# Hybrid decoder layer (HGRN2 and gated delta rule): one VectorE product moved two steps ahead in the delta loop, and one state load moved ahead in GpSimd's queue

## The chip, the cores and the metric

The kernel runs on one core of a Trainium2 chip. The metric is the device time in microseconds (us), the median of several runs; lower is better. Engines are named as in the profile: PE is TensorE (matmul) and PEld its weight load, DVE is VectorE, ACT is ScalarE, POOL is GpSimd, SP is the queue that issues the weight loads.

## The reference, cut to what matters

One inference step of one decoder layer, for a prompt of 256 tokens and for 8 samples of 4 tokens (288 token columns together), model width 2048, float32. An input projection feeds an HGRN2 branch (16 heads) and a gated-delta branch (16 query/key heads, 32 value heads of 128x128 state); the branches are merged, projected, and followed by a feed-forward block. Around the change stands the gated delta branch:

```python
conv = jax.nn.silu(conv)                         # causal width-4 convolution on q, k, v
beta = jax.nn.sigmoid(gb)
o_gdn, s_gdn_new = gdn_scan(q_g, k_g, v_g, log_a, beta, s_gdn.astype(f32))
o_gdn = rmsnorm(o_gdn, gdn_norm_g) * jax.nn.silu(gz.reshape(B, T, GDN_V_HEADS, GDN_DV))
...
X = lax.linalg.triangular_solve(A + eye, rhs, left_side=True, lower=True, unit_diagonal=True)
u, w = X[..., :GDN_DV], X[..., GDN_DV:]
v_new = u - jnp.einsum('bhtd,bhdv->bhtv', w, S)
```

`silu(gz)` is the output gate of the delta branch; `s_gdn` is the recurrent state that the samples bring along.

## The kernel before

Everything is transposed: 128 channels on the partitions, the 288 tokens as columns. A *slab* is one output block of 128 channels: 16 contraction tiles, each with three matmuls (`products`, L609 to L611), since float32 is split into a high and a low part (`hi*hi + lo*hi + hi*lo`). Weights come in *pieces* of 128x512: SP loads them in pairs into `raw` (8 pieces), ScalarE rounds them to `whi` (`split_hi`, L1036), VectorE subtracts to get `wlo` (`split_lo`, L1530); `whi` and `wlo` hold 4 pieces, and the splits run 3 pieces ahead of TensorE.

The heads' own work is woven by hand between the matmuls. Each slab has 8 *steps* `s`; the six slabs of one delta iteration have steps 0 to 47. For every step each engine's program says what it does there: `delta_first` and `delta_second` on TensorE, `delta_own` (the head pair `n+1` that is being projected) and `delta_prev` (the pair `n` whose scan runs) on ScalarE and VectorE; on both of these a step is `delta_prev`, then `delta_own`, then, at even steps, one weight split. Every engine works off its own program in order, and semaphores tie them together. There are 16 head pairs: an iteration without a scan (`S_G0`), eight iterations (`S_G1`), a stage of other slabs (`S_WB1`), seven iterations (`S_G2`), and the last pair's scan in the stage of the gates (`S_GB0`), where the split comes ahead of `delta_prev`.

The triangular solve is a chain of five levels. At level `l` TensorE makes `g_PU` (L799, at steps 4, 8, 11, 14, 17) from `glev` and `g_Ui`, ScalarE copies it, TensorE makes the correction (L812, and L815 for the samples), VectorE subtracts it from `g_Ui` (L1890, with L1889 for the samples, at steps 6, 10, 12, 16, 19) and transposes (L1893). GpSimd makes `glev` (L2338), the level's part of `g_A`.

The gate `silu(gz)` has two parts for each head pair. For the second, ScalarE computes the sigmoid at step 4 (`sigmoid_z(2 * n + 2)`), and VectorE multiplies at step 7 (`silu_z`, L1872, 128x288, both inputs in SBUF). Its result is read at step 42; it frees `g_ca` and `g_ce` for the convolution that starts at step 10. In between, at step 5, VectorE copies the halo of the convolution into `g_U` (L1774).

GpSimd runs its own program and issues DMAs in the same queue. In the stage `S_WA`, in which the HGRN2 output is projected, it stores finished blocks (`save`, L2239) and loads gates (`load_gate`, L2251); this stage also carries a share of the adaLN products, with weights of its own (`in_w_ada`). At its end GpSimd issues what the delta stage needs: `load_cache` (three small DMAs, L2277), `load_delta` (two DMAs of 512 KB, L2294, the samples' states `g_S0` of a head pair), `decay_rows` and `own` (which has the products L2317 and L2329). TensorE reads `g_S0` from step 9 of an iteration on.

Of the kernel before, what the change touches and what calls it, by code (L numbers as in the profile page):

```python
# [118 lines left out]
def hybrid_layer(nc, x_prompt, x_sample, state_hgrn, state_gdn, cache_conv, c_prompt, c_sample, lb_logits,  # L119
# [70 lines left out]
    with ExitStack() as ctx:  # L190
# [1251 lines left out]
        def _(dve):  # L1442
# [325 lines left out]
            def head(t, i, size=1):  # L1768
                return t[:, i:i + size] if isinstance(i, int) else t[:, bass.ds(i, size)]
# [99 lines left out]
            def silu_z(m, k):  # L1869

                dve.wait_ge(sg["g_zrec"], EARLIER + m)
                tt_(gz[:, k, :], gca[:, 0:T], gce[:, 0:T], MUL).then_inc(sg["g_z"], 1)  # L1872
# [1 line left out]
            UNEW = (6, 10, 12, 16, 19)  # L1874

            def delta_prev(s, n, slot):
                if s == 7:
                    silu_z(2 * n + 2, 1)
                if s == 12:
                    dve.wait_ge(sg["g_qws"], n + 1)  # L1880
                    tt_(guTs[:, :, :].rearrange("p e (b t) -> p e b t", t=TS), R[7][:, 64:128].rearrange("p (e b t) -> p e b t", e=2, t=TS),
                        gqws[:, :, :, 1, :], ADD).then_inc(sg["g_vt"], 1)
                if s in UNEW:
                    l = UNEW.index(s) + 1
                    dve.wait_ge(sg["g_ut"], 5 * n + l)
                    dve.wait_ge(sg["g_u1"], EARLIER + n + 1)
                    dve.wait_ge(sg["g_unew"], 5 * n + l - 1)
                    if l == 1:
                        tt_(gUs[0:NS, :, :], gUs[0:NS, :, :], R[4][0:NS, 0:2 * NS].rearrange("p (e s) -> p e s", s=NS), SUB)  # L1889
                    tt_(gUi[:, :, :], gUi[:, :, :], R[2][:, :].rearrange("p (q s) -> p q s", s=P), SUB).then_inc(sg["g_unew"], 1)  # L1890
                    if l < 5:
                        dve.wait_ge(sg["g_unew"], 5 * n + l)
                        flip(gT[:, :, :].rearrange("p q s -> p (q s)"), gUi[:, :, :].rearrange("p q s -> p (q s)")).then_inc(sg["g_tnew"], 1)  # L1893
                if s in (19, 23):
                    e = (s - 19) // 4
                    dve.wait_ge(sg["g_dss"], 2 * n + e + 1)
                    dve.wait_ge(sg["g_sdec"], 2 * n + e + 1)
                    for a in range(2):
                        h_ = gS0[:, e, 4 * a:4 * a + 4, :]
                        last = tt_(h_, h_, R[4 + a][:, :].rearrange("p (b v) -> p b v", v=P), ADD)  # L1900
                    last.then_inc(sg["g_snew"], 1)
                if s in DS:
                    c = DS.index(s)
                    dve.wait_ge(sg["g_ds"], 4 * n + c + 1)
                    dve.wait_ge(sg["g_o"], n)
                    dve.wait_ge(sg["g_stored"], 16 * n)
                    dve.wait_ge(sg["g_st"], 4 * n + c)
                    for e in range(2):
                        add = R[5][:, 2 * P * (c % 2) + e * P:2 * P * (c % 2) + (e + 1) * P]
                        if c == 0:  # L1910
                            last = copy(gS[:, 0, e, :], add)
                        else:
                            last = stt(gS[:, c, e, :], gS[:, c - 1, e, :], gsc[:, e, 9 + c:10 + c], add, MUL, ADD)
                    last.then_inc(sg["g_st"], 1)
                if s == 36:
                    dve.wait_ge(sg["g_ocp"], EARLIER + n + 1)
                    for e in range(2):
                        last = tt_(go[:, e, TP:T].rearrange("p (b t) -> p b t", t=TS),
                                   (R[7], R[4])[e][:, TP:T].rearrange("p (b t) -> p b t", t=TS), gqws[:, e, :, 0, :], ADD)
                    last.then_inc(sg["g_oadd"], 1)  # L1920
                if s == 42:
                    dve.wait_ge(sg["g_ors"], n + 1)
                    dve.wait_ge(sg["g_ohi"], n)
                    dve.wait_ge(sg["g_oadd"], EARLIER + n + 1)
                    dve.wait_ge(sg["g_z"], 2 * (n + 1))
                    stt(go[:, :, :], go[:, :, :], vec[:, 0, 6 * KT + 1:6 * KT + 2], gn1[:, :, :], MUL, MUL).then_inc(sg["g_ot1"], 1)
                    dve.wait_ge(sg["g_ot1"], EARLIER + n + 1)
                    tt_(gn2[:, :, :], go[:, :, :], gz[:, :, :], MUL).then_inc(sg["g_out"], 1)
                if s == 43:
                    dve.wait_ge(sg["g_ohi"], n + 1)  # L1930
                    tt_(head(olo, 2 * slot, 2), gn2[:, :, :], head(ohi, 2 * slot, 2).bitcast(F32), SUB).then_inc(sg["g_olo"], 1)

            def delta(at, j, n, slot):
                for s in range(49):
                    if n is not None:
                        delta_prev(s, n, slot)
                    delta_own(at, s, j)
                    if s % 2 == 0 and s < 48:
                        split_lo(at, s // 2)
# [12 lines left out]
            for s in range(49):  # L1952
                if s % 2 == 0 and s < 48:
                    split_lo(pos(S_GB0), s // 2)
                delta_prev(s, GJ - 1, HALF - 1)
# [176 lines left out]
        def _(pool):  # L2132
# [104 lines left out]
            def save(t, j, k):  # L2237

                pool.dma_start(scratch(t, j), pb[:, k, :]).then_inc(sg[f"t_stored{k}"], 16)  # L2239
# [16 lines left out]
            def merged_out(n):  # L2256
                at = pos(S_WA, n, 2)
                for k in range(2):
                    pool.wait_ge(sg[f"acc_free{at.bank(k)}"], at.drained(k))
                    save(merged_d, 2 * n - 2 + k, k)  # L2260
                    load_gate(2 * n + k, k)
# [5 lines left out]
            def conv_cols(t, j, c):  # L2267
                first, mul, size = cols[c]
                v = t.rearrange("r (c p) -> r c p", p=P)
                return v[:, first + mul * j:first + mul * j + size, :] if isinstance(j, int) else \  # L2270
                    v[:, bass.ds(first + mul * j, size), :]
# [3 lines left out]
            def load_cache(j):  # L2275
                for c in range(3):
                    pool.dma_start(gcc[0:24, places[c], :], conv_cols(cache_conv[0].rearrange("b s c -> (b s) c"), j, c)  # L2277
                                   ).then_inc(sg["g_cc"], 16)
# [8 lines left out]
            def pair_of(t, j):  # L2287

                v = t[0].rearrange("b (j e) d v -> j e d b v", e=2)
                return v[j] if isinstance(j, int) else v[bass.ds(j, 1)].squeeze(0)  # L2290

            def load_delta(j):
                for e in range(2):
                    pool.dma_start(gS0[:, e], pair_of(state_gdn, j)[e]).then_inc(sg["g_s0"], 16)  # L2294
# [77 lines left out]

            pool.wait_ge(sg["g_zero"], 1)
            load_cache(0)
            with pool.Fori(KT // 2 - 2, KT // 2) as n:
                merged_out(n)
            for k in range(2):
                at = pos(S_WA + KT - 2)
                pool.wait_ge(sg[f"acc_free{at.bank(k)}"], at.drained(k) + 1)
                save(merged_d, KT - 2 + k, k)  # L2380
            load_delta(0)
            pool.wait_ge(sg["g_halo_turned"], 1)
            load_cache(1)
            decay_rows(0)
# [89 lines left out]
```

## Time and profile before

| | |
|---|---|
| median of 3 runs | 3541.8 us (3540.53 to 3541.84) |
| the profiled execution: its own time | 3541.8 us |
| its span | 3540.3 us |
| TensorE, matmul | 98% busy |
| VectorE | 63% busy |
| ScalarE | 51% busy |
| GpSimd | 24% busy |
| delta iterations | 1012 to 1604 us and 1740 to 2255 us, the last scan to 2325 us |

The span is the profiled stretch from the first to the last instruction; 1.5 us lie around it. In a timeline row stand the start, the duration, the engine and line, the operation with what it writes and reads, and in brackets how long the engine had been idle before it and what ended that. A row with "x3" is three instructions in a row. Matmuls overlap, so a matmul of 0.29 us is followed by the next after 0.13 us.

### The profile page before, as it was taken

How to read it: one execution, taken by the hardware profiler on the slowest of the kernel's cores; microseconds unless marked ns; L12 is line 12 of the kernel's file. 1: busy time of each engine (PE TensorE's matmuls, PEld its weight loads, DVE VectorE, ACT ScalarE, POOL GpSimd, SP SyncE). 2: the span in 40 equal slices, each digit the busy share in tenths (PEclk: the TensorE clock that was granted, in tenths of full speed). 3: DMA queues.
4: the chain of work that ended last, by engine and by line, in shares of the span. 5: the costliest groups of instructions: out<-in, count | busy, mean ns of one | idle time of the engine just before them, and what ended most of it. 6: DMA issues, size and time to landing. Idle time of an engine off the chain costs nothing.

```text
span 3540.3 us, 76760 instructions
## 1 busy us (share of the span) xinstructions
PE 3475.6 (98%) x24605; PEld 3173.3 (90%) x24605; DVE 2236.2 (63%) x4307; ACT 1796.9 (51%) x3735; POOL 846.5 (24%) x995
## 2 busy tenths in 40 slices
PE   9999999999999999999999999999989999999998
PEld 2599999998889999998899999999879889999998
DVE  2476666746677777776677777646666665555555
ACT  1245454555545555556555555454665555344454
POOL 2122222211144554541254554412000000000000
PEclk9999999999999999999999999999999999999999
DMA  8755555567834443448744343468764775555554
GB/s 279 214 151 156 145 160 144 161 175 240 271 110 118 120 112 109 124 123 239 210 119 128 111 122 108 122 185 249 232 188 138 223 232 166 166 161 165 161 165 139
DMA packets 884547, 588.09 MB, mean 166 GB/s; under 512 B 23427, under 2 KB 816037, under 8 KB 884165
## 3 DMA queue, kind: packets, MB, share of 16 engines
q1 hardware_dynamic: 857828, 510.50, 50.5%
q0 software_dynamic: 26624, 76.41, 7.6%
q8 instruction: 50, 0.82, 0.1%
q14 instruction: 45, 0.36, 0.0%
HBM read 545.83 MB, written 40.99 MB: 166 GB/s over the span
## 4 chain that ended last, share of the span: by engine, by line
PE 69%; DVE 1%; issue 1%; ACT 1%; DVEq 0%; ACTq 0%
PE acc L609 18%; PE acc L611 17%; PE acc L610 17%; PE bank L799 2%; PE bank L812 2%; PE bank L849 2%; PE bank L833 1%; PE bank L621 1%; PE bank L622 1%; PE bank L870 1%; PE bank L881 1%; PE bank L895 1%; PE bank L771 1%; PE bank L742 1%; PE bank L747 0%
## 5 line engine op out<-in xcount | busy, mean ns | idle before, releaser
L1530 DVE TENSOR_TENSOR wlo<-raw,whi 128x512 fp32r<-128x512 f32 x1799 | 1304.7, 743 | 824.0 <-ACT whi L1036 809.8
L1036 ACT ACTIVATE whi<-raw 128x512 fp32r<-128x512 f32 x1799 | 1093.9, 627 | 838.6 <-PE acc L611 796.3
L609 PE MATMUL acc<-ahi,whi 128*128 128x288 f32 x4112 | 1288.3, 313 | 14.7 <-DVE alo L2041 9.1
L610 PE MATMUL acc<-alo,whi 128*128 128x288 f32 x4112 | 1214.7, 295 | 0.0
L611 PE MATMUL acc<-ahi,wlo 128*128 128x288 f32 x4112 | 1210.9, 294 | 0.0
L609 PEld LDWEIGHTS acc<-ahi,whi 128*128 128x128 f32 x4112 | 775.1, 188 | 37.4 <-issue 26.5
L610 PEld LDWEIGHTS acc<-alo,whi 128*128 128x128 f32 x4112 | 776.1, 189 | 13.3 <-issue 11.5
L611 PEld LDWEIGHTS acc<-ahi,wlo 128*128 128x128 f32 x4112 | 775.4, 189 | 0.0
L609 PE MATMUL acc<-ohi,whi 128*128 128x288 f32 x1792 | 532.7, 297 | 2.1 <-DVE wlo L1530 1.8
L610 PE MATMUL acc<-olo,whi 128*128 128x288 f32 x1792 | 529.3, 295 | 0.0
L611 PE MATMUL acc<-ohi,wlo 128*128 128x288 f32 x1792 | 527.9, 295 | 0.0
L609 PEld LDWEIGHTS acc<-ohi,whi 128*128 128x128 f32 x1792 | 336.6, 188 | 20.0 <-DVE wlo L1530 10.7
L610 PEld LDWEIGHTS acc<-olo,whi 128*128 128x128 f32 x1792 | 337.0, 188 | 2.9
L611 PEld LDWEIGHTS acc<-ohi,wlo 128*128 128x128 f32 x1792 | 337.8, 189 | 0.0
L2338 POOL TENSOR_TENSOR g_lev<-g_A,levm 128x512 f32<-128x512 f32 x80 | 114.8, 1435 | 264.3 <-DVE g_C L1795 220.1
L1787 DVE SCALAR_TENSOR_TENSOR g_ca<-g_U,g_cw,g_ca 128x312 f32<-128x312 f32 x192 | 130.3, 678 | 6.8
L1276 ACT ACTIVATE g_PU<-bank 128x512 f32<-128x512 f32 x80 | 47.9, 599 | 158.4 <-PE bank L799 147.7
L581 PE MATMUL acc<-raw,cst 128*9 128x512 f32 x256 | 116.7, 612 | 4.9 <-DVE cst L1461 2.5
L621 PE MATMUL bank<-whi,cs 128*18 128x512 f32 x256 | 101.4, 396 | 5.1 <-DVE wlo L1530 4.0
L1890 DVE TENSOR_TENSOR g_Ui<-g_Ui,bank 128x512 f32<-128x512 f32 x80 | 54.6, 683 | 80.1 <-PE bank L812 80.1
L581 PEld LDWEIGHTS acc<-raw,cst 128*9 128x9 f32 x256 | 22.4, 92 | 89.2 <-issue 72.0
L622 PE MATMUL bank<-wlo,cs 128*18 128x512 f32 x256 | 101.6, 397 | 0.0
(431 smaller groups left out, 4377.8 us busy)
## 6 DMA issues: line engine op xcount, KB each, us to landing
raw<-in_w_in SPq DMA_DIRECT2D x386, 512.0 KB, 4.1
raw<-in_w_ada SPq DMA_DIRECT2D x192, 512.0 KB, 4.6
raw<-in_w_up SPq DMA_DIRECT2D x128, 512.0 KB, 4.2
raw<-in_w_down SPq DMA_DIRECT2D x128, 512.0 KB, 4.0
raw<-in_w_out_gdn SPq DMA_DIRECT2D x64, 512.0 KB, 5.0
raw<-in_w_o SPq DMA_DIRECT2D x34, 512.0 KB, 4.7
raw<-in_w_out_hg SPq DMA_DIRECT2D x32, 512.0 KB, 5.5
g_S<-in_state_gdn POOLq DMA_DIRECT2D x32, 512.0 KB, 6.5
```

What stands on the lines that cost most here:

```text
L581: last = mm(acc[c % 2][0:NC, :], cst[:, 2 * l + a, :], raw[:, 2 * (l % 4) + a].rearrange("p k c -> p (k c)"), start=(l + a == 0), stop=(l ...
L609: mm(bank[:, 0:T], whi[:, s, r, :], hi[:, kt, :], start=(kt == 0), stop=False, skip_group_check=True)
L610: mm(bank[:, 0:T], whi[:, s, r, :], lo[:, kt, :], start=False, stop=False, skip_group_check=True)
L611: last = mm(bank[:, 0:T], wlo[:, s, r, :], hi[:, kt, :], start=False, stop=(kt == KT - 1), skip_group_check=True)
L621: mm(R[4][0:2 * NC, :], cs2[:, kt, :], whi[:, s].rearrange("p k c -> p (k c)"), start=(kt == 0), stop=False)
L622: mm(R[4][0:2 * NC, :], cs2[:, kt, :], wlo[:, s].rearrange("p k c -> p (k c)"), start=False, stop=(kt == KT - 1)).then_inc(sg["piece_used" ...
L799: last = mm(R[3][:, p * P:(p + 1) * P], glev[:, l % 2, p, :], gUi[:, p, :], start=True, stop=True)
L812: last = mm(R[2][:, p * P:(p + 1) * P], gT[:, p, :], gPU[:, p, :], start=True, stop=True)
L1036: f(whi[:, s], raw[:, r], ACT.Copy).then_inc(sg["hi_made"], 1)
L1530: tt_(wlo[:, s], raw[:, r], whi[:, s].bitcast(F32), SUB).then_inc(sg["lo_made"], 1)
L1787: stt(gca[:, 0:CW], gU[:, k, a:a + CW], gcw[:, k, a:a + 1], gca[:, 0:CW], MUL, ADD).then_inc(sg["g_part" if a < 3 else "g_tap"], 1)
L2338: last = pt(glev[:, l % 2], gA[:, :, :], levm[:, l, :].unsqueeze(1).to_broadcast([P, 4, P]), MUL)
```

## The change

Two edits. VectorE's `silu_z` of the second gate part stands at step 5 of `delta_prev` instead of step 7, so ahead of the halo copy of step 5 and of the update of `g_Us` and `g_Ui` at step 6. GpSimd's `load_delta(0)` stands right behind `load_cache(0)`, ahead of the last two passes of `merged_out` and of the last two saves, instead of behind them.

```diff
             def delta_prev(s, n, slot):
-                if s == 7:
+                if s == 5:
                     silu_z(2 * n + 2, 1)
                 if s == 12:
                     dve.wait_ge(sg["g_qws"], n + 1)
...
             pool.wait_ge(sg["g_zero"], 1)
             load_cache(0)
+            load_delta(0)
             with pool.Fori(KT // 2 - 2, KT // 2) as n:
                 merged_out(n)
             for k in range(2):
                 at = pos(S_WA + KT - 2)
                 pool.wait_ge(sg[f"acc_free{at.bank(k)}"], at.drained(k) + 1)
                 save(merged_d, KT - 2 + k, k)
-            load_delta(0)
             pool.wait_ge(sg["g_halo_turned"], 1)
             load_cache(1)
```

## Rows read from the trace of the kernel before

**Rows 1.** The page, part 1: busy time of each engine.
```profile
PE 3475.6 (98%) x24605; PEld 3173.3 (90%) x24605; DVE 2236.2 (63%) x4307; ACT 1796.9 (51%) x3735; POOL 846.5 (24%) x995
```

**Rows 2.** Waits of TensorE, 905 to 2330 us: total, times, longest.
```profile
PE acc L609 <- DVE wlo L1530: 3.7, 5, 1.4
PE bank L742 <- issue: 2.2, 2, 1.3
...
PE bank L799 <- DVE g_Ui L1890: 0.7, 1, 0.7
```

**Rows 3.** Timeline of VectorE, steps 4 to 7 of one delta iteration.
```profile
1238.59 1.76 DVE L1530 TENSOR_TENSOR wlo<-raw,whi 128x512 fp32r<-128x512 f32 x1 [2.07 <-ACT whi L1036]
1240.28 0.24 DVE L1774 COPY g_U<-bank 128x96 f32<-128x96 f32 x1
...
1240.57 0.67 DVE L1890 TENSOR_TENSOR g_Ui<-g_Ui,bank 128x512 f32<-128x512 f32 x1
...
1242.48 0.45 DVE L1872 TENSOR_TENSOR g_z<-g_ca,g_ce 128x288 f32<-128x288 f32 x1
1244.84 0.69 DVE L1530 TENSOR_TENSOR wlo<-raw,whi 128x512 fp32r<-128x512 f32 x1 [1.91 <-ACT whi L1036]
```

**Rows 4.** Timeline of TensorE, same iteration: step 8.
```profile
1241.77 1.05 PE L799 MATMUL bank<-g_Ui,g_lev 128*128 128x128 f32 x8
```

**Rows 5.** Timeline of GpSimd, same iteration.
```profile
1238.11 1.41 POOL L2329 TENSOR_TENSOR g_at<-g_GR,g_QKm 128x256 f32<-128x256 f32 x2
1239.49 0.31 POOL L2330 TENSOR_TENSOR g_ats<-g_GRs,g_QKms 32x64 f32<-32x64 f32 x1
1239.77 1.72 POOL L2338 TENSOR_TENSOR g_lev<-g_A,levm 128x512 f32<-128x512 f32 x1
```

**Rows 6.** Timeline of VectorE, step 16 of the last scan.
```profile
2280.91 0.67 DVE L1890 TENSOR_TENSOR g_Ui<-g_Ui,bank 128x512 f32<-128x512 f32 x1
```

**Rows 7.** Timeline of TensorE, same place.
```profile
2281.74 1.02 PE L799 MATMUL bank<-g_Ui,g_lev 128*128 128x128 f32 x7 [0.66 <-DVE g_Ui L1890]
```

**Rows 8.** Timeline of VectorE, one head of the HGRN2 stage.
```profile
312.12 0.68 DVE L1530 TENSOR_TENSOR wlo<-raw,whi 128x512 fp32r<-128x512 f32 x1
312.86 0.46 DVE L1665 TENSOR_TENSOR h_X<-h_q,h_E 128x288 f32<-128x288 f32 x1
313.24 1.07 DVE L1666 TENSOR_TENSOR h_X<-h_k,h_E 128x288 f32<-128x288 f32 x1
```

**Rows 9.** Timeline of GpSimd, same place.
```profile
312.91 1.08 POOL L2208 TENSOR_TENSOR h_X<-h_q,h_E 128x288 f32<-128x288 f32 x1 [6.56 <-ACT h_E L1119]
```

**Rows 10.** Timeline of VectorE, end of the first delta iteration.
```profile
1006.00 5.25 DVE L1530 TENSOR_TENSOR wlo<-raw,whi 128x512 fp32r<-128x512 f32 x1
1011.18 0.98 DVE L1872 TENSOR_TENSOR g_z<-g_ca,g_ce 128x288 f32<-128x288 f32 x1
```

**Rows 11.** Timeline of GpSimd, same place.
```profile
1010.67 1.17 POOL L2329 TENSOR_TENSOR g_at<-g_GR,g_QKm 128x256 f32<-128x256 f32 x1
```

**Rows 12.** Timeline of VectorE, end of the second delta iteration.
```profile
1084.21 0.44 DVE L1872 TENSOR_TENSOR g_z<-g_ca,g_ce 128x288 f32<-128x288 f32 x1
1084.58 0.67 DVE L1530 TENSOR_TENSOR wlo<-raw,whi 128x512 fp32r<-128x512 f32 x1
```

**Rows 13.** Timeline of GpSimd, same place.
```profile
1083.42 2.31 POOL L2317 TENSOR_TENSOR g_bek<-g_tk,g_sc 32x256 f32<-32x256 f32 x1
```

**Rows 14.** Timeline of VectorE, step 6 of the first iteration with a scan.
```profile
1018.39 0.21 DVE L1889 TENSOR_TENSOR g_Us<-g_Us,bank 32x64 f32<-32x64 f32 x1 [0.80 <-PE bank L815]
```

**Rows 15.** Timeline of VectorE, step 6 of an iteration in the second half.
```profile
1894.09 0.67 DVE L1890 TENSOR_TENSOR g_Ui<-g_Ui,bank 128x512 f32<-128x512 f32 x1
```

**Rows 16.** Timeline of TensorE, step 8 of the same iteration.
```profile
1895.39 0.83 PE L799 MATMUL bank<-g_Ui,g_lev 128*128 128x128 f32 x6
```

**Rows 17.** Timeline of VectorE, step 6 of the last scan.
```profile
2261.09 1.31 DVE L1530 TENSOR_TENSOR wlo<-raw,whi 128x512 fp32r<-128x512 f32 x1 [1.94 <-ACT whi L1036]
```

**Rows 18.** Timeline of GpSimd, same place.
```profile
2261.81 1.73 POOL L2338 TENSOR_TENSOR g_lev<-g_A,levm 128x512 f32<-128x512 f32 x1
```

**Rows 19.** Timeline of GpSimd, end of the stage S_WA.
```profile
909.85 1.54 POOL L2277 DMA_DIRECT2D g_cc<-in_cache_conv  x3
...
958.73 1.79 POOL L2294 DMA_DIRECT2D g_S<-in_state_gdn  x2
```

**Rows 20.** Busy times by stretch, then granted clock, DMA share, GB/s.
```profile
900.00:935.00 35.00, 34.30 (x231) 29.50 (x231) 23.23 (x39) 19.60 (x34) 5.89 (x11) 1.00 0.90 276
```

## The prediction

> **What bounds the kernel now.** I read the page first: TensorE is busy for 98% of the span [rows 1], so a gain or a loss counts only where it changes one of TensorE's rare gaps. Next came the waits of TensorE from 905 to 2330 us, the stretch that both edits touch. Its gaps there add up to 12.2 us in ten groups, 3.7 us of it for `wlo`, and one wait of 0.7 us, in the whole stretch, for VectorE's update of `g_Ui`, the tile beside which the first edit acts [rows 2]. So neither edit has much to win: even if all 12.2 us went, that would be 0.34% of 3541.8 us. The question is what either can lose. For that I read the timelines of VectorE, TensorE and GpSimd through one iteration of the delta loop (near 1240 us), compared the same place in all 16 iterations, and then looked for other places where VectorE and GpSimd overlap.
>
> **Edit 1: `silu_z(2n+2, 1)` from step 7 to step 5.** It is one `tensor_tensor` of 128x288 with both inputs in SBUF, 0.45 us, 16 times. At step 7 it stands behind the first update of `g_Ui`, at 1242.48 us, and VectorE is then free for 1.9 us until it waits for ACT [rows 3]. At step 5 it stands right behind the `wlo` split of step 4 (1238.59 to 1240.35 us) and ahead of the halo copy (`g_U`) and of the update of `g_Us` and `g_Ui` at step 6. ScalarE's `sigmoid_z` stands ahead of the `whi` piece that this split itself waits for, so no semaphore holds it up. Behind it in VectorE's queue is the `g_Ui` update, and for that TensorE waits: its second group of L799 (step 8) reads the new `g_Ui`.
>
> The slack of that update: it ends at 1240.57 + 0.67 = 1241.24 us and TensorE starts L799 at 1241.77, so 0.53 us [rows 3, 4]. From VectorE's end to TensorE's start when TensorE really waits takes 2281.74 - (2280.91 + 0.67) = 0.16 us [rows 6, 7]. So 0.37 us can be lost for nothing. An undisturbed silu_z takes this much and no more: the next instruction starts 0.37 us after it (1084.21 to 1084.58) [rows 12]. With nothing else in play, edit 1 costs about zero, by a hair.
>
> But GpSimd is in play. Its `g_lev` product (L2338, 128x512) is issued at 1239.77 us, while the split runs, and ends at 1241.49 [rows 5]. The split shows what overlap means: 1.76 us at 1238.59 against 0.68 where GpSimd is quiet [rows 3, 8], since it sat behind the two `g_at` products; it ran from about 1240.35 - 0.68 = 1239.67, and `g_lev`, issued 0.10 us later, waited in turn. Today the next VectorE operations (halo copy, `g_Us`, `g_Ui`) read PSUM and do not mind GpSimd: their 0.24 and 0.67 us are the same with and without it. silu_z has both inputs in SBUF. Who goes first, silu_z or the waiting `g_lev`? The trace of before has both answers.
>
> - GpSimd gets in between. In the HGRN stage L1665 runs from 312.86, GpSimd's L2208 is issued at 312.91, and the next VectorE product (L1666, the same shape as silu_z) takes 1.07 us instead of 0.46: it ends at 314.31, 0.32 us behind GpSimd's 313.99 [rows 8, 9]. This repeats in all 16 heads. And at 1011 us there is the very pair of the new order: a split that had been held up (5.25 us) ends at 1011.25, GpSimd's L2329 had been issued at 1010.67, 0.10 us after the split could start, and silu_z right behind took 0.98 us and ended at 1012.16, again 0.32 us behind GpSimd's 1011.84 [rows 10, 11].
> - VectorE keeps its turn. At 1083.42 GpSimd's L2317 is issued and takes 2.31 us, as a split, silu_z and a split run undisturbed in a row [rows 12, 13]; so in 15 iterations. There GpSimd's product was issued ahead of the first of the three.
>
> In the new place `g_lev` comes 0.10 us after the split could start: as at 1011 us, not as at 1083. I take the first answer. The chip has a rule for this too: the Trainium skill, SBUF — State Buffer, section "Who interferes with whom", says that a VectorE instruction with two SBUF inputs contends with a GpSimd instruction that reads SBUF, and that the second to issue blocks until the first is through. By that rule silu_z, issued at about 1240.28, stands behind `g_lev`, issued at 1239.77; the rows at 312 and 1011 us agree with it, the row at 1083.42 does not. With the rule the sum below comes out at 3557, without it at 3543.
>
> The price then: `g_lev` ends at 1241.49, as now; silu_z at 1241.49 + 0.32 = 1241.81; the halo copy starts 0.07 us before that, at 1241.74, where it starts at 1240.28 today. The shift is 1.46 us. TensorE waits 1.46 + 0.16 - 0.53 = 1.09 us. I find a slack of 0.53 us in five iterations and of 0.60 to 0.63 in seven (1895.39 - 1894.76 = 0.63 in one of them [rows 15, 16]), which makes 1.0 us in these; in one more VectorE has 0.2 us to spare and the wait is 0.8. Sum: 5 x 1.09 + 7 x 1.0 + 0.8 = 13.3 us. The first iteration of each half loop costs nothing: VectorE idles there for 0.80 us before `g_Us` [rows 14], and `g_lev` has already run. The last iteration (in the stage of the gates) has no slack (0.14 us) and another order: silu_z comes ahead of the `wlo` split that today starts at 2261.09 and takes 1.31 us under GpSimd's products [rows 17]. If silu_z runs into those products, the split comes later and can then fall behind `g_lev` of 2261.81 (1.73 us) [rows 18]; I bound it by 0.4 us (silu_z alone) and 1.7 us (behind `g_lev`), and take 1.3. Edit 1: 14.6 us. GpSimd itself is late for nobody: the product it makes at that point is needed some steps later.
>
> Nothing of this is won back at step 7: there VectorE only becomes idle sooner.
>
> **Edit 2: `load_delta(0)` earlier.** Two transfers of 0.52 MB, issued at 958.73 us today, go to about 911.4, right behind the `g_cc` loads of 909.85 [rows 19]. Nobody waits for them: the first reader is step 9 of the second delta iteration, the better part of 60 us behind today's issue. GpSimd pays 1.79 us of issuing, in a time when it waits for the next `pb`; the saves and gate loads behind it are two slabs ahead of their use. What it can cost is bandwidth: the stretch already moves 276 GB/s with the DMA engines 90% busy [rows 20]. Bounds: nothing, if the weights' lead (eight pieces of `raw`, up to four of `whi`/`wlo`) covers it; 1.05 MB / 276 GB/s = 3.8 us, if all of it goes ahead of weights and no lead covers any. I take 1 us, since ScalarE does wait for DMA there but TensorE mostly does not. A gain from a freer DMA after 958 us is bounded by the two waits for L742 that follow (2.2 us [rows 2]); they stand behind ScalarE's and VectorE's convolution work, not behind a transfer, so I take nothing.
>
> **Sum.** The profiled execution took 3541.8 us itself (span 3540.3), the same as the median. 3541.8 + 14.6 + 1.0 = 3557.4, rounded to 3557.
>
> **Rivals.**
> - *VectorE keeps its turn* (as at 1083 us): silu_z costs 0.37 us of shift, all of it slack; at most 0.08 us in each of five iterations and 0.4 us in the last. With edit 2 at 1 us: 3543, no change. The point that decides is whether silu_z in its new place takes 0.45 us or about 1.5. Chance 0.30.
> - *The early load starves the weights* and silu_z is harmless: up to 3.8 us of stalls near 911 to 925 us: 3546, no change within 0.2%. Chance 0.05.
> - *Faster*: what was late is relieved (the L742 gaps of 2.2 us, the 0.7 us wait for `g_Ui`): 3539, which is still no change; all 12.2 us would have to go for 3530. Chance 0.03 for a true gain, by something the trace does not show.
> - *The change does nothing*: if silu_z waited for its sigmoid and the order of VectorE's work stayed as it is; but ScalarE runs that sigmoid ahead of the `whi` piece for which the split of step 4 waits, so this can only be in the last iteration, where the order is another. Contained in the first rival.
>
> **How the numbers follow.** The likeliest case (0.62) gives 3557, with its own range 3551 to 3561: the last iteration and edit 2 at either bound, and 0.1 us on each of 13 waits. The range must take in the no-change case as well: 3541 to 3561. 0.2% (7 us) is what a measurement can tell here. Slower 0.63, same 0.34, faster 0.03.
>
> **What would show it.** Right: L1872 has 13 or so instances of about 1.5 us; TensorE's waits list L799 behind `g_Ui` 13 or 14 times with 1.0 to 1.1 us each; GpSimd's `g_lev` there still takes 1.72 us. Wrong: L1872 stays at 0.45 us and `g_lev` grows to about 2.1 us. Edit 2 is right if the load lands near 920 us and TensorE's gaps from 905 to 960 us grow by no more than 2 us. The prediction fails if the arbitration between the two engines goes by something else than the order of issue, or if the split of step 4 no longer overlaps `g_lev`.

## The result, and the profile after

The changed kernel took 3562.58 us (median of 4 runs, 3558.65 to 3563.32), the kernel before 3541.16 us beside it (4 runs, 3535.44 to 3541.84): a ratio of 1.0064, 95% interval [1.005, 1.0079], 21.4 us slower. The forecast was 3557 us with 3561 at the top of the range: the direction and the mechanism of edit 1 came out as forecast, and the time lies 1.6 us above the range. The forecast was 15.6 us over the 3541.8 us of the time before. The profiled execution took 3563.5 us, with a span of 3562.0 us against 3540.3, 21.7 us more.

The page, part 1, answers to [rows 1]: TensorE is still busy for 98% of a longer span. VectorE's busy time grew by 16.5 us, the first sign of instructions that are held up while they count as running.

```profile
PE 3481.4 (98%) x24605; PEld 3176.9 (89%) x24605; DVE 2252.7 (63%) x4307; ACT 1796.9 (50%) x3735; POOL 845.4 (24%) x995
```

The waits of TensorE from 905 to 2360 us (total, times, longest), which answer to [rows 2]:

```profile
PE bank L799 <- DVE g_Ui L1890: 13.6, 15, 1.5
PE acc L609 <- ACT g_C L1045: 3.3, 1, 3.3
PE acc L609 <- DVE wlo L1530: 2.4, 4, 1.4
PE bank L747 <- DVE wlo L1530: 2.3, 2, 1.1
PE bank L742 <- issue: 2.2, 2, 1.3
```

The wait for `g_Ui` went from 0.7 us once to 13.6 us in 15 waits, the forecast's main sign (one of the 15 is the old one, 0.65 us at 2303.5 us); the wait for L742 is what it was. The 3.3 us behind `g_C` is new, and 1.1 of the 2.3 us at L747 too. VectorE in the iteration of [rows 3], now 3.8 us later:

```profile
1242.41 1.77 DVE L1530 TENSOR_TENSOR wlo<-raw,whi 128x512 fp32r<-128x512 f32 x1 [2.06 <-ACT whi L1036]
1244.10 1.54 DVE L1872 TENSOR_TENSOR g_z<-g_ca,g_ce 128x288 f32<-128x288 f32 x1
1245.56 0.24 DVE L1774 COPY g_U<-bank 128x96 f32<-128x96 f32 x1
...
1245.86 0.67 DVE L1890 TENSOR_TENSOR g_Ui<-g_Ui,bank 128x512 f32<-128x512 f32 x1
```

GpSimd in the same place, answering to [rows 5]:

```profile
1243.32 0.31 POOL L2330 TENSOR_TENSOR g_ats<-g_GRs,g_QKms 32x64 f32<-32x64 f32 x1
1243.60 1.72 POOL L2338 TENSOR_TENSOR g_lev<-g_A,levm 128x512 f32<-128x512 f32 x1
```

`g_lev` still takes 1.72 us and ends at 1245.32; silu_z takes 1.54 us in place of 0.45 and ends at 1245.64, 0.32 us behind it, as the two models at 312 and 1011 us had it [rows 8 to 11]. The halo copy starts 3.15 us behind the split's start, where it was 1.69 us [rows 3]: the shift is the forecast's 1.46 us. Of the 16 silu_z in the new place, 13 take 1.53 to 1.55 us; the first of each half loop takes 0.45 us (1019.30 and 1756.00 us), the one in the last scan 3.09 us.

TensorE's timeline of after, six instructions (the load's stretch, the first L734, the same step 8 as in [rows 4], the last scan):

```profile
921.35 0.40 PE L609 MATMUL acc<-ohi,whi 128*128 128x288 f32 x1 [3.28 <-ACT g_C L1045]
...
962.34 0.60 PE L734 MATMUL bank<-ident,g_cc 128*128 128x128 f32 x4
...
1246.67 1.13 PE L799 MATMUL bank<-g_Ui,g_lev 128*128 128x128 f32 x8 [0.93 <-DVE g_Ui L1890]
...
2274.46 1.05 PE L799 MATMUL bank<-g_Ui,g_lev 128*128 128x128 f32 x8
...
2281.93 1.13 PE L799 MATMUL bank<-g_Ui,g_lev 128*128 128x128 f32 x8 [1.49 <-DVE g_Ui L1890]
...
2292.03 1.05 PE L799 MATMUL bank<-g_Ui,g_lev 128*128 128x128 f32 x8
```

The counterparts of the second, fourth, fifth and sixth of these in the kernel before, the same matmuls:

```profile
960.37 0.60 PE L734 MATMUL bank<-ident,g_cc 128*128 128x128 f32 x4
...
2257.26 1.05 PE L799 MATMUL bank<-g_Ui,g_lev 128*128 128x128 f32 x8
...
2263.26 1.13 PE L799 MATMUL bank<-g_Ui,g_lev 128*128 128x128 f32 x8
...
2270.19 1.13 PE L799 MATMUL bank<-g_Ui,g_lev 128*128 128x128 f32 x8
```

Subtract, and the 21.7 us fall into five pieces. One more pair of the same matmul (an L621 at 883.02 us before, 881.00 after) gives the first:

| stretch (time of before) | shift at its end | share |
|---|---|---|
| up to 883 us | -2.02 | -2.0 |
| 883 to 960: stage with the early load | +1.97 | +4.0 |
| 960 to 2257: the delta iterations | +17.20 | +15.2 |
| 2257 to 2263: the wait in the last scan | +18.67 | +1.5 |
| 2263 to 2270: right behind it | +21.84 | +3.2 |

**The first piece is not the change's.** The profiled execution of before had an interruption of its own: a TensorE wait of 2.30 us at 838.77 us, and a granted clock of 0.88 in the ten microseconds from 840, where after has 1.00. Both kernels run the same code there. In the ten other profiled executions the same matmul too comes 0.7 to 4.5 us earlier than in before. My sum was made against 3541.8 us, which held these 2 us; in the runs beside the experiments below the kernel before takes 3537.7 to 3538.7 us.

**The piece of the early load.** GpSimd issues it at 908.57 us, and ScalarE then gets its next pieces of weights late; timeline of GpSimd, then of ScalarE:

```profile
908.57 1.84 POOL L2294 DMA_DIRECT2D g_S<-in_state_gdn  x2
```

```profile
912.73 1.15 ACT L1036 ACTIVATE whi<-raw 128x512 fp32r<-128x512 f32 x2 [1.04 <-DMA raw<-in_w_ada]
...
919.67 1.15 ACT L1036 ACTIVATE whi<-raw 128x512 fp32r<-128x512 f32 x2 [3.85 <-DMA raw<-in_w_out_hg]
920.73 0.57 ACT L1045 ACTIVATE g_C<-bank 18x512 f32<-18x512 f32 x1
```

TensorE's wait is put down to `g_C`, but the engine that makes `g_C` had itself waited 3.85 us for the DMA of `raw`: that is where the 3.28 us come from. Stretches of after (busy us of PE, PEld, DVE, ACT, POOL, then granted clock, DMA share, GB/s); the first answers to [rows 20]:

```profile
900.00:935.00 35.00, 31.67 (x203) 27.17 (x202) 20.17 (x34) 17.27 (x30) 6.64 (x11) 0.95 0.90 276
910.00:920.00 10.00, 8.07 (x55) 6.84 (x53) 4.37 (x7) 3.47 (x7) 1.53 (x3) 1.00 1.06 311
920.00:930.00 10.00, 8.65 (x51) 7.96 (x52) 5.31 (x10) 4.87 (x9) 1.08 (x2) 0.83 0.76 241
...
2280.00:2290.00 10.00, 8.51 (x49) 8.31 (x48) 3.50 (x6) 3.36 (x7) 5.62 (x9) 0.70 0.29 77
```

In the kernel before, the second of these:

```profile
910.00:920.00 10.00, 10.00 (x70) 8.85 (x69) 7.07 (x12) 6.49 (x12) 2.50 (x5) 1.00 0.96 279
```

Over 35 us the DMA share is 0.90 and the rate 276 GB/s in both kernels. Over the ten microseconds in which the load runs they are 1.06 and 311 GB/s, where before had 0.96 and 279: there was little room left there even without the load. TensorE's clock is granted at 0.83 in the stretch behind the wait, 1.7 of the 4.0 us of this piece, and at 0.70 behind the 1.49 us wait of the last scan (1.00 in before in both). Of its two levels, 2.4 and 1.2 GHz, TensorE had the lower for a part of these stretches, behind a wait in each case.

**The last scan.** VectorE, then GpSimd, answering to [rows 17, 18]:

```profile
2276.28 3.09 DVE L1872 TENSOR_TENSOR g_z<-g_ca,g_ce 128x288 f32<-128x288 f32 x1
2279.30 1.77 DVE L1530 TENSOR_TENSOR wlo<-raw,whi 128x512 fp32r<-128x512 f32 x1
```

```profile
2276.80 0.61 POOL L2317 TENSOR_TENSOR g_kls<-g_tk,g_sc 32x256 f32<-32x256 f32 x1
2277.37 1.40 POOL L2329 TENSOR_TENSOR g_at<-g_GR,g_QKm 128x256 f32<-128x256 f32 x2
2278.74 0.32 POOL L2330 TENSOR_TENSOR g_ats<-g_GRs,g_QKms 32x64 f32<-32x64 f32 x1
```

silu_z does not get in between GpSimd's products at all: it ends at 2279.37, behind the chain up to `g_ats` (2279.06) by 0.31 us.

### The profile page after: what moved, and what is told of

The parts are those of the page before. It is cut to its first block, busy times and chain, and to the rows that moved or that the text cites. A ratio compares the mean times of both kernels' runs of the same rounds, so it can differ in the third digit from the quotient of the medians.

```text
span 3562.0 us, 76760 instructions
## 1 busy us (share of the span) xinstructions
PE 3481.4 (98%) x24605; PEld 3176.9 (89%) x24605; DVE 2252.7 (63%) x4307; ACT 1796.9 (50%) x3735; POOL 845.4 (24%) x995
## 4 chain that ended last, share of the span: by engine, by line
PE 93%; DVE 3%; issue 2%; DMA 1%; ACT 1%; DVEq 0%; POOL 0%; ACTq 0%; SPq 0%; POOLq 0%
PE acc L609 23%; PE acc L611 22%; PE acc L610 22%; PE acc L581 3%; PE bank L799 2%; PE bank L812 2%; PE bank L849 2%; PE bank L833 1%; PE bank L621 1%; PE bank L622 1%; DMA raw<-in_w_ada 1%; PE bank L870 1%; PE bank L674 1%; PE bank L676 1%; DVE wlo L1530 1%
## 5 line engine op out<-in xcount | busy, mean ns | idle before, releaser
L610 PEld LDWEIGHTS acc<-alo,whi 128*128 128x128 f32 x4112 | 776.6, 189 | 13.3 <-issue 11.5
L609 PEld LDWEIGHTS acc<-ohi,whi 128*128 128x128 f32 x1792 | 336.7, 188 | 22.6 <-DVE wlo L1530 10.0
L621 PE MATMUL bank<-whi,cs 128*18 128x512 f32 x256 | 101.3, 396 | 3.4 <-DVE wlo L1530 2.5
L799 PE MATMUL bank<-g_Ui,g_lev 128*128 128x128 f32 x640 | 87.9, 280 | 16.6 <-DVE g_Ui L1890 13.6
```

What stands on the lines that cost most here:

```text
L609: mm(bank[:, 0:T], whi[:, s, r, :], hi[:, kt, :], start=(kt == 0), stop=False, skip_group_check=True)
L610: mm(bank[:, 0:T], whi[:, s, r, :], lo[:, kt, :], start=False, stop=False, skip_group_check=True)
L621: mm(R[4][0:2 * NC, :], cs2[:, kt, :], whi[:, s].rearrange("p k c -> p (k c)"), start=(kt == 0), stop=False)
L799: last = mm(R[3][:, p * P:(p + 1) * P], glev[:, l % 2, p, :], gUi[:, p, :], start=True, stop=True)
```

## Experiments

Each stands beside runs of the kernel before on the same chip, whose medians were 3538.39 us (e1 to e4), 3538.72 (e5 to e8) and 3537.72 (e9, e10).

| run | edit | us (median, runs) | over before | ratio, 95% interval |
|---|---|---|---|---|
| e1 | edit 1 alone | 3555.14 (5) | +16.8 | 1.0049 [1.0035, 1.0062] |
| e2 | edit 2 alone | 3544.89 (11) | +6.5 | 1.002 [1.0011, 1.0029] |
| e3 | PSUM copy of that length instead | 3540.08 (10) | +1.7 | 1.0004 [0.9995, 1.0013] |
| e4 | edit 1, `g_lev` later | 3543.68 (10) | +5.3 | 1.0016 [1.0006, 1.0025] |
| e5 | edit 1 but for the last scan | 3553.8 (5) | +15.1 | 1.004 [1.0026, 1.0054] |
| e6 | half of edit 2 | 3542.67 (11) | +4.0 | 1.0007 [0.9998, 1.0016] |
| e7 | edit 2, 32 us later | 3544.65 (11) | +5.9 | 1.0016 [1.0007, 1.0025] |
| e8 | `g_lev` later alone | 3539.91 (10) | +1.2 | 1.0002 [0.9992, 1.0011] |
| e9 | both edits again | 3560.29 (5) | +22.6 | 1.0066 [1.0052, 1.008] |
| e10 | edit 1, two products | 3563.34 (4) | +25.6 | 1.0069 [1.0053, 1.0084] |

**e1 and e2: each edit alone.**

```diff
e1: -                if s == 7:
    +                if s == 5:
e2: +            load_delta(0)          (behind load_cache(0))
    -            load_delta(0)          (behind the last saves)
```

> Edit 1 alone (silu_z at step 5, the load where it was). Theory (silu_z sits behind GpSimd's g_lev 13 times, each time TensorE waits 0.9 to 1.2 us more, and the last scan loses about 4.6 us with a fall of the clock): 3541.2 + 17 to 18 = 3558 to 3560, L1872 at about 1.5 us in 13 instances. Rival (the early load does most of it, the iterations pay less than the waits say because slack elsewhere gives some back): under 3552.

> Edit 2 alone (load_delta(0) early, silu_z at step 7). Theory (1.05 MB share the DMA engines with the weights where these are 90% busy; TensorE stalls once by about 3.3 us and its clock falls after that): 3541.2 + 4 to 5 = 3545 to 3546, one wait of 3 us or more near 918 us. Rival (the stall at 918 us is an accident of one execution, the load is hidden): 3541 to 3542, no wait above 1 us there.

The two differences of medians, 16.8 and 6.5 us, add to 23.3 where both together cost 21.4 to 22.6: they add up. TensorE's waits, e1 and then e2, and e2's other wait in the same stretch:

```profile
PE bank L799 <- DVE g_Ui L1890: 13.6, 15, 1.5
```

```profile
PE acc L609 <- ACT g_C L1045: 2.8, 1, 2.8
...
915.23 0.40 PE L609 MATMUL acc<-ohi,whi 128*128 128x288 f32 x1 [1.66 <-DVE wlo L1530]
```

e1 has the 13.6 us and no wait for `g_C`, e2 has the wait for `g_C` and still the old 0.7 us for `g_Ui`. e2 refutes my "about 1 us" for the load: its trace loses 5.0 us against before from 883 to 960 us (L621 at 878.51, L734 at 960.88 us), where the profiles without a load there move by -1.1 to +0.6 us, and 1.1 us more at L747, 6.1 us in all, close to the 6.5 us of the medians.

**e3: as long on VectorE, but not on the shared input.** A copy of 128x288 from PSUM into a spare tile at step 5; silu_z stays at step 7.

```diff
+                    copy(spare[:, :], R[7][:, 0:T])
```

> Kernel before, with one more VectorE instruction at step 5, in the place where edit 1 puts silu_z: a copy of 128x288 from PSUM into a spare tile, which takes as long as silu_z (0.45 us) but reads only PSUM. silu_z stays at step 7. Theory (it is the second SBUF input that meets GpSimd): the copy takes 0.45 us, the g_Ui update moves by 0.37 us, inside its slack, TensorE waits for g_Ui no more than 0.1 us an iteration: 3541 to 3543. Rival (any VectorE work of this length ahead of g_Ui costs TensorE about 1 us an iteration): 3553 to 3557.

VectorE of e3, at the place of [rows 3] (its lines stand one or two later):

```profile
1236.78 0.45 DVE L1775 COPY spare<-bank 128x288 f32<-128x288 f32 x1
1237.15 0.24 DVE L1776 COPY g_U<-bank 128x96 f32<-128x96 f32 x1
```

The copy takes 0.45 us while GpSimd's `g_lev` runs from 1236.28 to 1238.01 beside it, and TensorE's wait for `g_Ui` stays at 0.7 us, once. So the slack does cover an undisturbed operation of this length, and silu_z's own 0.37 us is not the cost. What is left is the wait behind `g_lev`.

**e4: edit 1 with `g_lev` moved away,** and **e8: that move alone.** GpSimd issues the three `g_cc` loads first and `g_lev` behind them, 1.6 us later.

```diff
-                level(n, 3)
                 if cache:
                     pool.wait_ge(sg["g_halo_turned"], n + 2)
                     load_cache(n + 2)
+                level(n, 3)
```

> Edit 1 alone, and GpSimd's order changed in prev: load_cache is issued ahead of the product g_lev of level 3 instead of behind it, so that in the 14 iterations with a load_cache no GpSimd product waits beside the split of step 4. Theory: silu_z at step 5 then takes 0.45 us in these iterations and TensorE's waits for g_Ui go from 13 or 14 to 2 (the two iterations without load_cache): 3541 + 5.5 to 6 = 3546 to 3548. Rival (silu_z at step 5 is slow for another reason, its sigmoid for one): no change against edit 1 alone, 3558 to 3560.

> Control: silu_z at step 7 and the load late, as before, but load_cache ahead of g_lev of level 3 in GpSimd's queue. Theory (that order matters only for a VectorE product with two SBUF inputs beside it, and TensorE waits for none of them before): 3537 to 3542, the same as before, so the gain of that order in the run with edit 1 is all from silu_z. Rival (the order is a gain by itself): 3534 or less.

VectorE, then GpSimd, of e4 in the same iteration:

```profile
1236.04 0.81 DVE L1530 TENSOR_TENSOR wlo<-raw,whi 128x512 fp32r<-128x512 f32 x1 [2.06 <-ACT whi L1036]
1236.77 0.97 DVE L1872 TENSOR_TENSOR g_z<-g_ca,g_ce 128x288 f32<-128x288 f32 x1
```

```profile
1235.56 1.86 POOL L2329 TENSOR_TENSOR g_at<-g_GR,g_QKm 128x256 f32<-128x256 f32 x2
1237.39 0.53 POOL L2330 TENSOR_TENSOR g_ats<-g_GRs,g_QKms 32x64 f32<-32x64 f32 x1
```

With `g_lev` gone, silu_z does not get the 0.45 us that I had expected. It falls behind the next product that GpSimd has waiting, here the second of the two `g_at`: that one ends at 1237.42, silu_z at 1237.74, again 0.32 us behind. It takes 0.97 or 0.98 us in 11 of the 16 places, 0.45 in two, 1.53 in two and 3.09 in the last scan. Most of the 0.97 is slack, and TensorE's waits for `g_Ui` are 3.3 us in 4 times. Edit 1's cost falls from 16.8 to 5.3 us, and e8 shows that the move has no gain of its own to lend. In the 11 places the product beside which silu_z lands sets its price. One place does not fit: at 1088.28 us silu_z takes 1.53 us and ends 1.28 us behind the last product of GpSimd, while GpSimd only issues the three `g_cc` loads. The trace does not say what it waited for.

**e5: the last scan at step 7.**

```diff
-                if s == 5:
+                if s == (7 if isinstance(n, int) and n == GJ - 1 else 5):
```

> Edit 1 alone in all iterations, but in the last scan (stage of the gates) silu_z stays at step 7. Theory (the last scan pays its own 1.5 us, as silu_z waits there for a chain of GpSimd products, and up to 3.1 us more in executions in which the clock then falls): 1.5 to 3 us below edit 1 alone, so 3552 to 3557; one wait for g_Ui of 1.5 us fewer, 12 or 13 waits of 0.6 to 1.0 us left. Rival (the last scan has slack elsewhere): no change against edit 1 alone.

TensorE's waits of e5:

```profile
PE bank L799 <- DVE g_Ui L1890: 12.2, 14, 1.0
```

One wait of 1.5 us less, as expected; by medians 15.1 us against e1's 16.8, a difference inside the two intervals.

**e6 and e7: how much of the load, and when.** e6 issues one of the two transfers early; e7 issues both ahead of the last two saves, at 940.59 us.

```diff
e6: +            load_delta(0, (0,))    (behind load_cache(0))
    +            load_delta(0, (1,))    (behind the last saves)
e7: +            load_delta(0)          (ahead of the last two saves)
```

> Edit 2 with only the first of the two transfers of 0.52 MB early, the second where it was. Theory (bandwidth: the stall is the transfer's time less a lead of the weights): the wait near 918 us falls from about 3 us to 1.5 us or less, the clock keeps 1.00 behind it, and the time is 3539 to 3543. Rival (it is the interruption of GpSimd's queue or of the gate loads that costs, whatever the size): the same wait of about 3 us.

> load_delta(0) whole, between the last pass of merged_out and the last two saves, near 944 us: 33 us later than in edit 2, 14 us ahead of where it was, when SP has issued the last of the adaLN weights. Theory (what counts is that the weights want 90% of the DMA engines while the load runs; behind the last adaLN piece they want less): no wait above 1.5 us, 3538 to 3542, as before. Rival (any place in the stage S_WA starves the weights alike): a wait of about 3 us, 3543 or more.

e6 waits 0.2 us for `g_C`, once; ten microseconds of it, at the load (columns as above):

```profile
910.00:920.00 10.00, 9.14 (x61) 7.39 (x60) 5.97 (x11) 5.09 (x9) 1.11 (x2) 1.00 1.09 326
```

ScalarE of e7:

```profile
951.28 1.15 ACT L1036 ACTIVATE whi<-raw 128x512 fp32r<-128x512 f32 x2 [5.33 <-DMA raw<-in_w_out_hg]
```

TensorE of e7 (start, then the wait ahead of it in brackets):

```profile
952.68 0.40 PE L609 MATMUL acc<-ohi,whi 128*128 128x288 f32 x1 [3.39 <-DVE wlo L1530]
```

I had tied the stall to the projections of the modulation near 918 us and expected none behind them. That fell: the same load 32 us later makes ScalarE wait 5.33 us for `raw` and TensorE 3.39 us. It holds the weights up at both places tried. Whether half the size is cheap is less clear. In e6's trace TensorE hardly waits for the half load (0.2 us, against 2.8 to 3.4 us with 1.05 MB), although the DMA share of 1.09 is as high as in after. But that trace is of the fastest of e6's 11 executions (3538.96 us), as e7's is (3541.10), and by medians half the load still costs 4.0 us and the whole, late, 5.9 us; these runs cannot tell the two apart.

**e9: the changed kernel again.**

> The changed kernel itself once more, on another chip and in more rounds, to see how firm the 21.4 us are. The profiled executions and the two edits alone put it at 15 to 17 us for edit 1 and 4 to 6.5 us for edit 2. The theory (the two costs add up): 19 to 23 us over the kernel before, ratio 1.0055 to 1.0065. The rival (the first measurement was a high draw and my forecast of 15.6 us stands): ratio 1.0044 or below. Beside that: whether TensorE's granted clock falls again after the wait at 2282 us (0.70 in the 10 us behind it in the first profile); if it stays at 1.00 there, the fall belongs to an execution and not to the change.

Waits of TensorE of e9, then its TensorE in the last scan, then the stretch behind it:

```profile
PE bank L799 <- DVE g_Ui L1890: 13.3, 15, 1.5
...
PE acc L609 <- ACT g_C L1045: 3.1, 1, 3.1
```

```profile
2280.93 1.13 PE L799 MATMUL bank<-g_Ui,g_lev 128*128 128x128 f32 x8 [1.51 <-DVE g_Ui L1890]
...
2287.85 1.13 PE L799 MATMUL bank<-g_Ui,g_lev 128*128 128x128 f32 x8
```

```profile
920.00:930.00 10.00, 10.00 (x62) 9.32 (x63) 5.07 (x11) 4.20 (x7) 1.09 (x2) 0.83 0.69 209
...
2280.00:2290.00 10.00, 9.07 (x76) 9.05 (x77) 4.07 (x8) 3.48 (x8) 6.05 (x9) 1.00 0.26 73
```

The cost of 22.6 us stands, so the first measurement was no high draw: it is 7.0 us more than the forecast's difference of 15.6. The same wait (1.51 us) now leaves the clock at 1.00, and the next L799 comes 6.92 us later as in before (6.93), not 10.10 us: the 3.2 us of the last piece belong to one execution, not to the change each time. The 0.83 at 920 us comes back, as it does in e2.

**e10: two products in a row.** Edit 1, and ahead of silu_z a second product of the same inputs.

```diff
+                if k == 1:
+                    tt_(spare[:, :], gca[:, 0:T], gce[:, 0:T], MUL)
                 tt_(gz[:, k, :], gca[:, 0:T], gce[:, 0:T], MUL)
```

> Edit 1 alone, and with it a second product of the same two inputs, written to a spare tile ahead of the real one, at step 5 in all 16 iterations: VectorE then has two 128x288 SBUF products between the split and the halo copy. The theory (GpSimd's g_lev, issued while the split runs, gets in once, behind the split, and blocks only what is next): the first product takes about 1.5 us and the second about 0.45; the shift is 1.46 + 0.37 us, TensorE waits 1.35 to 1.5 us in each of 13 iterations, and the kernel takes 4.8 to 5.5 us more than with edit 1 alone, 21 to 23 us over the kernel before. The rival (whoever holds the port keeps it through a row of products, so that with two VectorE products in a row g_lev loses its turn, as L2317 does at 1083 us): both products take 0.45 us, g_lev 2.5 us, shift 0.8 us, wait 0.4 us or less, 5 us or less over the kernel before.

VectorE of e10, the same iteration; then the waits of its TensorE; then the wait ahead of one of its five falls of the clock, and the stretch of that fall:

```profile
1241.36 1.54 DVE L1874 TENSOR_TENSOR spare<-g_ca,g_ce 128x288 f32<-128x288 f32 x1
1242.82 0.45 DVE L1875 TENSOR_TENSOR g_z<-g_ca,g_ce 128x288 f32<-128x288 f32 x1
```

```profile
PE bank L800 <- DVE g_Ui L1893: 19.0, 15, 1.9
```

```profile
1319.50 1.13 PE L800 MATMUL bank<-g_Ui,g_lev 128*128 128x128 f32 x8 [1.33 <-DVE g_Ui L1893]
...
1320.00:1330.00 10.00, 10.00 (x60) 10.00 (x59) 3.19 (x7) 2.36 (x6) 5.03 (x8) 0.66 0.27 78
```

`g_lev` gets in once and blocks the first product only; the second takes its 0.45 us. The waits grow by 19.0 - 13.6 = 5.4 us, inside the 4.8 to 5.5 expected; the median grows by more (25.6 against 16.8 us, with wide intervals; the two fastest of the four runs, 3560.22 and 3560.57 us, are 22.5 and 22.9 us over before). Its profiled execution was the slowest, 3574.03 us, and its clock was granted at 0.94 in five stretches of 60 us of the delta iterations and the last scan, the one around the row above among them. At 0.66 over ten microseconds a fall costs 3.4 us, so five of them explain why this execution stands 13.8 us above the fastest.

## Why the prediction was wrong, point by point

- **GpSimd gets in between:** right. The 1.46 us of shift, the 0.32 us between the two ends and the unchanged `g_lev` are as forecast; e3, e4 and e10 show that they are the cause. Of the 16 silu_z moved, 13 fell behind `g_lev`, the last one (3.09 us) behind a chain of other products of GpSimd, and the first of each half loop met none (0.45 us). Where `g_lev` was waiting, VectorE never kept its turn, which was the rival with 0.30.
- **13.3 us in 13 iterations:** right for the waits. Measured by when TensorE starts L799 behind the matmul ahead of it (0.13 to 0.14 us before, 1.21 us at 1246.67 after), the delays are 0.77, 1.01, five of 1.07 to 1.08, and six of 0.97 to 1.11 us, 13.4 us. I left out what follows a wait: the next group (L823) starts 0.97 us behind L799 instead of 0.88, some 0.09 x 13 = 1.2 us. Together with a new wait of 1.1 us at L747 that makes 15.7, close to the 15.2 us of that stretch. The first iteration of each half cost nothing, as forecast.
- **The last scan, 1.3 us:** 1.5 us (e1, e5), by another way than either bound: silu_z took 3.09 us behind a whole chain of GpSimd's products, and the split behind it 1.77 us.
- **Edit 2, 1.0 us: this step failed.** It said that TensorE mostly does not wait for DMA there. That was true of before and no statement about a queue with 1.05 MB more in it. The wait is 2.8 to 3.3 us and, with the clock of 0.83 behind it, the piece is 4.0 us in the profile and 6.5 us by e2's median. The upper bound of 3.8 us held for the longest stall alone: e2 has 2.8 and 1.7 us in two waits, 4.5 in all. The extra 1.1 us at L747, which shows only in profiles with a load right behind `load_cache(0)`, is counted to this edit too. Its row, a DMA share of 0.90 over 35 us, had no room to take 3.8 us of transfer unseen; the mean hid that ten microseconds of it, at the place of the load, stood at 0.96 already. I also held "the load starves the weights" as a rival *instead of* edit 1's cost, with 0.05, when the two are independent and add.
- **The range was added up wrongly.** By its own terms it is 3541.8 + (13.3 - 1.3) + 0.4 + 0 = 3554.2 to 3541.8 + (13.3 + 1.3) + 1.7 + 3.8 = 3561.9 us, not 3551 to 3561. The measured time lies 0.7 us above that too.
- **TensorE's clock was in no term.** The sum took a wait of TensorE to cost its own length. Behind waits of 2.8 us and more at 918 us it cost more in three profiles of three (0.83 each time), behind e7's 3.39 us at 952.68 the clock stayed at 1.00; behind the 1.5 us waits of the last scan once 3.2 us and twice nothing (e1, e9); behind e10's waits of 1.3 to 1.9 us five times 3.4 us and otherwise nothing. With edit 2 at 4 to 6.5 us and the last scan as measured, the same working gives 3541.8 + 13.3 + 1.5 + 4 to 6.5 = 3560.6 to 3563.1, which holds the 3562.58. That fit is partly luck: it leaves out the 1.2 us behind the waits, and it starts 3 to 4 us above what the kernel before takes in the later runs.
- **Not settled.** The extra 1.1 us at L747 shows in each profile with the load, or half of it, right behind `load_cache(0)` (after, e2, e6, e9), and in no other; no run shows a link between them. Why `g_lev` wins here and L2317 at 1083 us loses three times in a row [rows 12, 13] stays open too: e10 shows that it is not the number of VectorE products in a row. No version beat the kernel before.

## What to carry to other kernels

Before moving a VectorE product with two SBUF inputs, look on GpSimd's timeline for a product issued while the VectorE instruction ahead of the new place runs: it got in first in 13 of 13 such places here, and the price was its remaining length, not that of the product moved. A copy from PSUM in the same place cost nothing that the runs can tell from zero (+1.7 us, e3). A prefetch that "nobody waits for" was charged to the weights that share the DMA engines: look at stretches as short as the transfer, not at the stage's mean, and ask how many bytes the consumer's pieces in flight can cover.

## What the runs showed of the hardware that was not expected

- Either engine can be the one that waits through several products of the other. VectorE was kept waiting through a chain of GpSimd products (3.09 us instead of 0.45 at 2276.28 in after; 5.25 us at 1006.00 in before [rows 10]), and GpSimd through three VectorE products (2.31 us [rows 13]). The Trainium skill, SBUF — State Buffer, section "Who interferes with whom", has an exclusive lock that the second to issue waits for; the 13 cases of 1.54 us agree, the product of 2.31 us at 1083.42, issued first, does not.
- A DMA share near 1 does not by itself say that TensorE stalls: with 1.05 MB more it waited 2.8 to 3.4 us at a time (after, e2, e7, e9), with 0.52 MB more, at a share of 1.09, 0.2 us in the one execution traced, and by medians e6 still lost 4.0 us.
- The granted clock can fall behind a wait of 1.5 us (0.70 over the next ten microseconds, 3.2 us lost) or not (1.00 in e9), in the same kernel at the same instruction; in e10 it fell behind five of its waits of 1.3 to 1.9 us, at 3.4 us each. So one execution can stand well above the others of the same kernel: e10's profiled one is 13.8 us above its fastest.
